# Hybrid decoder step: the prompt's probability copies moved up in each step, sample rows transposed in whole pieces

## The reference, cut to what matters

```
h = rmsnorm(x) ; z = h @ w_in                 # 1024 x 2840, split into
qa | kv_c, kv_s | kv_w, gates | qb | kb | vb  # queries and K/V of two mixers, 8 heads each
A: compressed, selected and window attention, gated (2 K/V heads, 4 query heads each)
B: dilated attention, (window, step) = (128,1), (512,4), (2048,16), joined by their sums
x = x + concat(A, B) @ w_out
x = x + square(relu(rmsnorm(x) @ w_up)) @ w_down
```

## Time and profile before

| | |
|---|---|
| median of 3 runs | 2379.99 us (2376.47 to 2381.29) |
| the profiled execution | 2381.06 us, span 2379.2 us |
| TensorE (PE) busy | 2273.5 us, 96% of the span |
| VectorE (DVE) busy | 893.0 us, 38% |
| ScalarE (ACT) busy | 563.7 us, 24% |
| GpSimd (POOL) busy | 645.3 us, 27% |
| TensorE clock, mean granted | 0.988 |

### The profile page before, as it was taken

How to read it: one execution, slowest core, us unless ns; L and a number is a source line. 1 busy time by engine, 2 the same in 40 slices (tenths; PEclk the granted TensorE clock), 3 DMA queues, 4 the chain that set the end, 5 groups by cost and what they waited for, 6 DMA issues and landing times.

```text
span 2379.2 us, 43924 instructions
## 1 busy us (share of the span) xinstructions
PE 2273.5 (96%) x13772; PEld 1622.8 (68%) x13772; DVE 893.0 (38%) x2370; ACT 563.7 (24%) x1356; POOL 645.3 (27%) x719
## 2 busy tenths in 40 slices
PE   7999889999999999999999998999999999999998
PEld 4545557776766777777755455667776777777776
DVE  2002663434354222336510146443434532223374
ACT  2101661111113322120111036411111233122202
POOL 0001761101043344334200037510101434334341
PEclk8999999999999999999999999999999999999999
DMA  9542016787864444444365320188788534544441
GB/s 352 205 165 79 20 54 232 262 325 260 328 254 164 160 170 183 165 173 185 137 261 199 121 74 0 64 285 322 263 326 283 219 136 184 199 177 183 165 165 40
DMA packets 129685, 448.23 MB, mean 188 GB/s; under 512 B 19074, under 2 KB 90755, under 8 KB 108419
## 3 DMA queue, kind: packets, MB, share of 16 engines
q1 hardware_dynamic: 118768, 416.45, 47.8%
q10 hardware_dynamic: 10770, 29.98, 3.7%
HBM read 435.76 MB, written 152.57 MB: 247 GB/s over the span
## 4 chain that ended last, share of the span: by engine, by line
PE 88%; issue 4%; DVE 4%; ACT 2%; DMA 1%; DVEq 0%; ACTq 0%; SPq 0%; POOLq 0%
PE bank L1067 38%; PE bank L1150 14%; PE bank L1364 10%; PE bank L1432 3%; PE bank L1540 3%; PE bank L1311 2%; PE bank L1299 2%; PE bank L1331 2%; PE bank L1163 1%; PE bank L1486 1%; PE bank L1565 1%; ACT zone L704 1%; PE bank L1048 1%; PE bank L1512 1%; PE bank L1542 1%
## 5 line engine op out<-in xcount | busy, mean ns | idle before, releaser
L1067 PE MATMUL bank<-zone,ring 128*128 128x288 f32 x1664 | 425.1, 407 | 11.4 <-DVE zone L1705 8.8
L1067 PEld LDWEIGHTS bank<-zone,ring 128*128 128x128 f32 x1664 | 315.2, 190 | 104.7 <-DVE zone L1705 14.3
L1067 PE MATMUL bank<-zone,w 128*128 128x288 f32 x1408 | 353.5, 406 | 0.0
L1150 PE MATMUL bank<-ring,hT 128*128 128x512 f32 (+2 forms) x800 | 340.4, 580 | 6.4 <-ACTq L749 5.0
L1067 PEld LDWEIGHTS bank<-zone,w 128*128 128x128 f32 x1408 | 267.5, 190 | 73.9
L1150 PEld LDWEIGHTS bank<-ring,hT 128*128 128x128 f32 (+1 forms) x800 | 150.9, 194 | 164.7 <-issue 153.3
L873 POOL TENSOR_TENSOR w<-ring 128x512 f32<-128x512 f32 x72 | 95.6, 1328 | 554.5 <-PE bank L1067 314.0
L1364 PE MATMUL bank<-ring,w 128*128 128x128 f32 x2048 | 242.5, 277 | 0.0
L1364 PEld LDWEIGHTS bank<-ring,w 128*128 128x128 f32 x2048 | 233.0, 192 | 3.9 <-issue 3.8
L611 ACT COPY zone<-bank 128x288 f32<-128x288 f32 x72 | 28.6, 397 | 568.9 <-PE bank L1067 568.9
L986 POOL TENSOR_TENSOR zone<-constants,stat 128x1024 f32<-128x1024 f32 x16 | 30.3, 1896 | 457.7 <-DVE stat L2062 457.7
(11 more groups left out here) (258 smaller groups left out, 2811.6 us busy)
## 6 DMA issues: line engine op xcount, KB each, us to landing
out_dil_s<-in_state_kv_dil SPq DMA_DIRECT2D x48, 2720.0 KB, 12.0
ring<-in_w_units SPq DMA_DIRECT2D x72, 1024.0 KB, 4.9
zone<-in_dilated_v SPq DMA_DIRECT2D x16, 3072.0 KB, 12.1
ring<-in_cache_kv_cmp SPq DMA_DIRECT2D x256, 128.0 KB, 2.2
ring<-in_cache_kv_sel SPq DMA_DIRECT2D x256, 128.0 KB, 6.2
ring<-in_w_in SPq DMA_DIRECT2D x10, 2048.0 KB, 8.2
zone<-in_dilated_k SPq DMA_DIRECT2D x16, 1280.0 KB, 5.8
zone<-in_dilated_k SPq DMA_DIRECT2D x16, 1024.0 KB, 7.9
```

What stands on the lines that cost most here:

```text
L1067: last = mm(dst[:, 0:HALF], lhs[:, k, :], rhs(k), start=first and k == 0, stop=(k == 3), skip_group_check=True)
L1150: last = mm(dst, hT[:, k, t * P:t * P + ROWS[t]], ring[:, n % 2, k * CH:k * CH + width], start=start and k == 0, stop=stop and k == KT - 1)
```

## The change

Five edits:

1. ScalarE's `prompt_steps`: `keep_first_head` of step m - 3 stands before `step_probs` of step m.
2. VectorE's `prompt_steps`: `keep_second_head` of step m - 3 stands directly behind `step_bias` of step m, before the reciprocal of step m - 1 and all else of the step.
3. The halves of the sample rows' chunks are contiguous for qb and kb; for qa each half holds two of the four query heads of both K/V heads. So every 128 staged columns hold both 64-wide halves of a pair, and `sample_transposes` turns them with two whole 128 by 128 transposes.
4. `z_keep` reads the transposed sample rows in the new layout (`of_half`); for qb it does so in four instructions in place of two.
5. The sample rows' keys of kb are stored with two DMAs in place of eight.

```diff
-Z_STORES_S = {**Z_STORES, "wg": 2, "kb": 8}
+Z_STORES_S = {**Z_STORES, "wg": 2, "kb": 2}
...
                     if kind == "kb":
-                        for h in range(8):
-                            put("dil", (h // 2 * HD, h // 2 * HD + HD), h * HD, h * HD + HD, (low, high)[h % 2])
+                        put("dil", (0, 256), 0, 256, low)
+                        put("dil", (0, 256), 256, 512, high)
...
                 for m in range(first, last):
+                    if m >= TO_T and (m - TO_T < STEPS or not ends):
+                        keep_first_head(l, *in_round(g, m - TO_T))
                     if m < STEPS or not ends:
                         step_probs(l, *in_round(g, m))
                     if m == 6:
                         act.wait_ge(c_b.sem, c_b.at(l, g + 1))
                         nc.scalar.activation(p_c, p_c, ACT.Exp).then_inc(c_e.sem, 1)
-                    if m >= TO_T and (m - TO_T < STEPS or not ends):
-                        keep_first_head(l, *in_round(g, m - TO_T))
...
-                        if Z_CHUNKS[c][0] in ("qb", "kb"):
-                            columns = w.rearrange("p (g k d) -> p k g d", g=4, k=2)[:, e]
-                        else:
-                            columns = w[:, a:z]
-                        last = mm(B[rows, 0:z - a], hT[:, k, SEQ:TOK], columns, start=(k == 0), stop=(k == KT - 1),
+                        out, columns = B[rows, 0:z - a], w[:, a:z]
+                        if Z_CHUNKS[c][0] == "qa":
+                            out = out.rearrange("p (g k d) -> p g k d", g=2, k=2)
+                            columns = w.rearrange("p (k g d) -> p g k d", g=4, k=2)[:, 2 * e:2 * e + 2]
+                        last = mm(out, hT[:, k, SEQ:TOK], columns, start=(k == 0), stop=(k == KT - 1),
...
                 if kind in ("qa", "qb", "kb"):
-                    for j in range(4):
-                        tr(B[low, j * P:j * P + 64], s[low, j * HD:(j + 1) * HD], ident[low, low])
-                        last = mm(B[high, j * P:j * P + 64], s[high, j * HD:(j + 1) * HD], ident[high, high])
+                    for j in range(2):
+                        last = tr(B[:, j * P:(j + 1) * P], s[:, j * P:(j + 1) * P], ident[:])
...
+                of_half = B[:, 0:2 * P].rearrange("p (j e c) -> p e j c", j=2, e=2)
...
-                    last = V.tensor_copy(knb[:], by4[:, :, 0:64])
+                    last = V.tensor_copy(knb[:].rearrange("p (e j) c -> p e j c", e=2), of_half)
...
-                            last = V.tensor_scalar(qdb[rows, :, :, :, k].rearrange("p q b t -> p q (b t)"),
-                                                   by4[rows, :, 0:64], SCALE, None, ALU.mult)
+                            for e in range(2):
+                                last = V.tensor_scalar(qdb[rows, 2 * e:2 * e + 2, :, :, k].rearrange("p q b t -> p q (b t)"),
+                                                       of_half[rows, e], SCALE, None, ALU.mult)
...
                     if m < STEPS or not ends:
                         step_bias(l, *in_round(g, m))
+                    if m >= TO_T and (m - TO_T < STEPS or not ends):
+                        keep_second_head(l, *in_round(g, m - TO_T))
                     if m >= 1 and (m - 1 < STEPS or not ends):
                         step_weights(l, *in_round(g, m - 1))
...
-                    if m >= TO_T and (m - TO_T < STEPS or not ends):
-                        keep_second_head(l, *in_round(g, m - TO_T))
```

More of the change, by code:

```diff
@@ L1804, in z_keep @@
                                 last = V.tensor_scalar(qd[rows, :, 32 * k + 8 * g:32 * k + 8 * g + 8],
-                                                       by4[rows, g, 0:64].rearrange("p (b t) -> p b t", b=NB),
+                                                       of_half[rows, g // 2, g % 2].rearrange("p (b t) -> p b t", b=NB),
                                                        SCALE, None, ALU.mult)
                         else:
-                            last = V.tensor_scalar(qdb[rows, :, :, :, k].rearrange("p q b t -> p q (b t)"),
-                                                   by4[rows, :, 0:64], SCALE, None, ALU.mult)
+                            for e in range(2):
+                                last = V.tensor_scalar(qdb[rows, 2 * e:2 * e + 2, :, :, k].rearrange("p q b t -> p q (b t)"),
+                                                       of_half[rows, e], SCALE, None, ALU.mult)
                 last.then_inc(z_te.sem, 1)
```

## The result

| | before | after |
|---|---|---|
| median | 2379.9 us (2376.47 to 2381.29, 4 executions) | 2346.02 us (2342.1 to 2352.48, 4 executions) |
| ratio | | 0.9862, 95% interval 0.9836 to 0.9889 |
| profiled execution | 2381.06 us, span 2379.2, clock 0.988 | 2352.48 us, span 2350.6, clock 0.988 |

The change makes the kernel 1.4% faster. The profiled execution of after is the slowest of its four. Against the execution on which the sum was made it is 28.6 us faster, where 28.7 were predicted; the medians are 33.9 us apart. The median of after is 6.5 us lower than its profiled execution; the four have mean granted clocks of 0.988, 0.990, 0.991 and 0.992 in the order of their times, 2352.48, 2348.37, 2343.67 and 2342.1. Where TensorE's clock falls for some microseconds differs from execution to execution, so I compare stages of a profile in which it does not fall, and take totals last.

A forecast was written before the change was run, and what follows sets the result against it. TensorE, holding 88% of the chain that ended last, was taken as the bound; projection 13.2 us plus attention 15.5 gave 28.7, so 2381.06 - 28.7 = 2352.4 us, with an eight-in-ten range of 2344 to 2367.

The forecast's parts named there:

- The transposes: Projection, sample rows of qa, qb and kb: two whole transposes replacing eight small operations save 9.8 us, bounds 8.4 to 11.1.
- The clock: Projection, product behind kb: with less small work before it, 7.06 us instead of 8.76, 3.4 us over both layers.
- Rival (b): Projection: TensorE's clock still falls behind kb, so 3.4 us are not gained and the time is 2355.8 us; chance 0.09.
- The rest of the projection: Column order, kb's fewer stores and VectorE's moves of sample rows: together 0, bounds -0.7 and +0.7 us.
- ScalarE's copy: Prompt attention: TensorE's 32 waits for this copy, 23.4 us, go, except where another engine is next late.
- GpSimd at the round's end: Prompt attention: GpSimd's weighting makes TensorE wait 1.31 us instead of 1.04 at six round ends, taking back 7.3 us.
- the 0.6 kept for the start of each layer's rounds: Prompt attention: the first exponentials come late anyway, so 0.3 us a layer is deducted from the gain.
- rival (a): Prompt attention: TensorE waits for VectorE's copy or GpSimd at the same instants, attention brings 0, 2367.9 us; chance 0.13.
- the predicted 15.5: Prompt attention's whole gain in us: 23.4 of waits less 7.3 at round ends and 0.6 at layer starts.
- The slower rival: Prompt attention: weighting, transposes, VectorE's copy and reciprocal form a loop of 6.47 us per two steps, 2386.8 us; chance 0.04.

## Why the prediction was right

**The transposes** (predicted 9.8): 132.91 - 128.04 = 4.87 a layer, 9.8. 0.22 for two and 6.87 behind them, as taken. The kernels with four small pairs put back give the price of the small pairs from the other side, 1.71 a set.

**The clock** (3.4): gained in full, 9.87 to 8.17 in both layers and in every kernel without the small pairs (12 passages). The outcome was right, the reason less firm than I wrote: I took a fall seen 2 times in 2 for a rule, and a length of small work near it gave none in 6. Rival (b) did not come about: with 1.33 us there was never a fall.

**The rest of the projection** (0): the stage is shorter by the transposes alone, and eight stores in place of two change nothing.

**ScalarE's copy** (all 23.4 gone): gone. The exponentials don't start later: 0.73 behind line 1848's start (250.23 - 249.50), where it was 0.74.

**GpSimd at the round's end** (a wait of 1.31 in place of 1.04, 7.3 us taken back): the mechanism was right and the size a little off. The wait is 0.60 + 0.54 = 1.14, twelve waits and 6.9 us in all. I let VectorE's copy delay GpSimd by its whole 0.27; GpSimd started 0.20 later, and TensorE's wait grew by 0.10. The loss at an end is 0.94 + 0.10 = 1.04, six of them 6.2 us, not 7.3. I had also placed it wrongly: half of the wait comes one step earlier, behind the second pass, and only half behind the last.

**What I did not see**: VectorE's copy of step 5's transposes (256 columns) is late by 0.40, and TensorE's second-head transposes of step 6 wait for it: 6 times, 2.4 us ("issue" in the list). The copy and the transposes that wait for it:

```profile
242.64 0.42 DVE L1867 COPY zone<-bank 128x256 f32<-128x256 f32 x1
...
243.16 0.52 PE L1310 MATMUL bank<-c_ident,zone 128*128 128x128 f32 x3 [0.40 <-issue]
```

It replaces waits on ScalarE at the same instants, so a part of rival (a) is real: 2.4 of the 23.4 us. **What I counted too low**: the stage's windows give TensorE's idle time as 170.24 - 155.47 = 14.77 before and 161.86 - 154.75 = 7.11 after; 7.66 a layer or 15.3 in both, which is the predicted 15.5. The other 1.4 us is busy time, 0.72 a layer, that no step of mine has; what makes the same 1203 instructions busy for less I did not settle. So among the waits three errors nearly cancel: a loss at the round's ends that was 1.1 too large, the 0.6 kept for the start of each layer's rounds, of which nothing came, and the unseen 2.4 the other way. The 0.5 that is left are small waits that I did not follow up. That the waits came out at 15.3 for 15.5 is in part luck.

**The slower rival** (d), the ring through VectorE: a round takes 30.02 us and not more than before, so the ring did not close, and the attention is faster in every kernel that has both copies moved.

**The total and the median.** 28.6 for 28.7 is luck as well: the attention brought 1.25 more than its 15.5, and the stretches without changed code took 1.3 back. The median came out 6.5 us below the profiled execution, where I expected 1. The three other executions have the higher mean clock (0.990 to 0.992 for 0.988), so the likely cause is how often the clock fell; only the profiled one has a trace, so this is not shown. The median, 2346.02, lies inside the range because that was wide for other reasons, and near its lower bound of 2344.

## What to carry to other kernels

When two engines each free one of two buffers that a third waits for, look at both: moving the late one pays alone, moving the other pays only after it, and tried in the wrong order it looks worthless. Before a wait is taken away, time the next engine's route from the same event to the same consumer; here it was 0.1 us behind and took back about a quarter of the gain, and that engine's slow instruction form was then worth another 9.9 us. Many small operations in a row cost TensorE their own time and can cost the clock of the large product behind them; whether they do is to be seen from several executions, not from one (5 of 6 and 0 of 6 passages here for nearly the same length).

## What the runs showed of the hardware

**GpSimd's scaling by one scalar operand is the slow form.** 128 x 512: 1562 ns with one, 775 with two; at 384 columns 1242 and 664, at 256 922 and 557, at 128 768 and 666. The Trainium skill, page "GPSIMD Engine Reference", section "3.1 Elementwise — side-by-side cycle accounting", gives 769 ns for 512 elements in its best loop; the form with two operands agrees with 775, and the form with one is at twice that. The selected and window steps, whose second operand is the gate, take 975 in after and 944 in before. The kernel with ones as the second operand is the fastest here: 2332.08 us, ratio to before 0.9806, and 0.6% under the changed kernel's median: 13.9 us, of which the attention stages show 9.9.

**The same kernel differs by 10 us from execution to execution on one core**, 2342.1 to 2352.48 for after, in step with the mean granted clock. A profile is one draw of it: stage times without a fall repeat far better over executions and kernels: 128.03 to 128.04 for the projection and 8.17 to 8.18 behind kb in six kernels, and 161.80 to 161.96 for the attention, but for the two stages at 162.3. They are what small edits should be judged by.
